# Seven row blocks of each feed-forward output projection computed as 2x2 block products with seven multiplications (Strassen's scheme, Winograd's form), block sums on GpSimd

## The reference, cut to what matters

```python
D_MODEL, D_FF, SEQ = 1024, 2816, 256

def swiglu(x, w_in, w_out):
    gate, up = jnp.split(x @ w_in, 2, axis=-1)
    return (jax.nn.silu(gate) * up) @ w_out

for i in range(2):
    h = h + 0.5 * swiglu(rmsnorm(h, norm_g[i, 0]), ffn_w_in[i, 0], ffn_w_out[i, 0])
    h = h + mixer(rmsnorm(h, norm_g[i, 1]))        # mixer_a for i = 0, mixer_b for i = 1
    h = h + 0.5 * swiglu(rmsnorm(h, norm_g[i, 2]), ffn_w_in[i, 1], ffn_w_out[i, 1])
return rmsnorm(h, final_g)
```

## Time and profile before

| | before |
|---|---|
| median of 3 runs | 1740.37 us (1740.19 to 1740.73) |
| span of the profiled execution | 1738.4 us |
| outside the span, against the median | 2.0 us |
| PE busy | 1722.3 us, 99% |
| DVE busy | 870.7 us, 50% |
| ACT busy | 659.1 us, 38% |
| POOL busy | 37.3 us, 2% |
| granted PE clock, mean | 0.998 |

### The profile page before, as it was taken

How to read it: one execution, slowest core, us unless ns; L and a number is a source line. 1 busy time by engine, 2 the same in 40 slices (tenths; PEclk the granted TensorE clock), 3 DMA queues, 4 the chain that set the end, 5 groups by cost and what they waited for, 6 DMA issues and landing times.

```text
span 1738.4 us, 21080 instructions
## 1 busy us (share of the span) xinstructions
PE 1722.3 (99%) x9024; PEld 1294.2 (74%) x9024; DVE 870.7 (50%) x1138; ACT 659.1 (38%) x831; POOL 37.3 (2%) x64
## 2 busy tenths in 40 slices
PE   9999999999999999999999999999999999999998
PEld 7988744444444458888998888888888899888887
DVE  6876411111111146554686555465546688565554
ACT  5555311111111144443335444344434444444442
POOL 2010000000000000000000000000001000000000
PEclk9999999999999999999999999999999999999999
DMA  9738999999999995554743555545556654545551
GB/s 357 215 129 315 356 409 427 428 429 429 425 431 425 426 391 198 194 185 140 265 146 113 196 187 194 193 183 193 181 186 220 220 188 146 191 172 206 183 183 46
DMA packets 50756, 439.02 MB, mean 253 GB/s; under 512 B 6368, under 2 KB 6764, under 8 KB 11616
## 3 DMA queue, kind: packets, MB, share of 16 engines
q1 hardware_dynamic: 46640, 425.17, 64.0%
q0 software_dynamic: 3792, 12.15, 2.5%
q10 hardware_dynamic: 224, 0.29, 0.0%
HBM read 434.37 MB, written 3.15 MB: 252 GB/s over the span
## 4 chain that ended last, share of the span: by engine, by line
PE 96%; DMA 1%; DVE 1%; issue 1%; ACT 1%; POOLq 0%; POOL 0%; DVEq 0%; ACTq 0%
PE PS L629 22%; PE PS L631 22%; PE PS L630 22%; PE PS L1874 18%; PE PS L1841 3%; PE PS L1932 2%; DMA ujug<-in_wt 1%; PE PS L2581 1%; PE PS L668 1%; PE PS L3115 1%; PE PS L1912 1%; PE PS L2723 0%; DMA ki<-ki 0%; PE PS L1006 0%; PE PS L2759 0%
## 5 line engine op out<-in xcount | busy, mean ns | idle before, releaser
L587 DVE TENSOR_TENSOR wl<-ring,wh 128x2048 fp32r<-128x2048 f32 (+1 forms) x207 | 470.1, 2273 | 284.7 <-ACT wh L578 284.5
L578 ACT ACTIVATE wh<-ring 128x2048 fp32r<-128x2048 f32 (+1 forms) x207 | 393.5, 1902 | 274.5 <-PE PS L631 274.5
L629 PE MATMUL PS<-wh,XTh 128*128 128x512 f32 x952 | 378.3, 397 | 1.9 <-DVE wl L623 0.6
L631 PE MATMUL PS<-wh,XTl 128*128 128x512 f32 x952 | 371.5, 390 | 0.0
L630 PE MATMUL PS<-wl,XTh 128*128 128x512 f32 x952 | 371.0, 390 | 0.0
L629 PEld LDWEIGHTS PS<-wh,XTh 128*128 128x128 f32 x952 | 178.8, 188 | 39.3 <-issue 1.2
L631 PEld LDWEIGHTS PS<-wh,XTl 128*128 128x128 f32 x952 | 178.7, 188 | 38.2
L630 PEld LDWEIGHTS PS<-wl,XTh 128*128 128x128 f32 x952 | 179.0, 188 | 35.1 <-issue 0.2
L629 PE MATMUL PS<-XTh,wh 128*128 128x256 f32 (+2 forms) x480 | 137.8, 287 | 0.1
L629 PE MATMUL PS<-wh,hTh 128*128 128x512 f32 x352 | 137.6, 391 | 0.0
L631 PE MATMUL PS<-wh,hTl 128*128 128x512 f32 x352 | 137.1, 389 | 0.0
(11 more groups left out here) (460 smaller groups left out, 1913.4 us busy)
## 6 DMA issues: line engine op xcount, KB each, us to landing
ring<-in_wt SPq DMA_DIRECT2D x205, 1024.0 KB, 4.9
ubuc<-in_wt SPq DMA_DIRECT2D x6, 4096.0 KB, 22.8
uf<-in_wt SPq DMA_DIRECT2D x20, 1024.0 KB, 20.4
uhui<-in_wt SPq DMA_DIRECT2D x5, 4096.0 KB, 24.3
ujug<-in_wt SPq DMA_DIRECT2D x5, 4096.0 KB, 21.4
uaue<-in_wt SPq DMA_DIRECT2D x5, 4096.0 KB, 23.6
uaue<-in_wt SPq DMA_DIRECT2D x9, 2048.0 KB, 21.3
ud<-in_wt SPq DMA_DIRECT2D x9, 2048.0 KB, 23.8
```

The lines of the kernel that those rows point to most:

```text
L578: s.activation(k.pieces(i)[0], k.raw(i), ACT.Copy).then_inc(*k.w_hi.up(i))
L587: v.tensor_tensor(l, k.raw(i), h.bitcast(F32), ALU.subtract).then_inc(*k.w_lo.up(i))
L629: pe.matmul(o, lhsT=left[0], rhs=right[0], start=first, stop=False)
L631: return pe.matmul(o, lhsT=left[1], rhs=right[0], start=False, stop=final)
```

## The change

Of the eleven parts of each output projection, parts 1 to 7 (`QUADS`) are computed as one 2 x 2 block product: left the two halves of the tokens by the two blocks of 128 rows, right the part cut into four blocks of 128 x 512. Seven products take the place of eight. For this

- the host packs the four blocks of such a part in another order (`quad`); the part is as large as before,
- GpSimd makes four sums of the right blocks (`sum_blocks`: one instruction over 128 x 1024, two over 128 x 512, each waiting for the one before) into one of two places `sums0`, `sums1`; the third and later of a stage wait until the sums two before have been split,
- ACT and DVE split three of the four blocks (1536 columns instead of 2048) and all the sums (another 2048): two items, which take two of the three split places in turn (`items`),
- GpSimd makes four sums of the left blocks (`sum_forms`, 128, 256 and 128 columns), and ACT and DVE split seven forms of 128 columns instead of four blocks (896 columns instead of two times 256),
- the seven products go to the four old banks and to four more, which had held gate and up (`quad_banks`), and are collected there over the seven parts,
- before the tail ACT copies one of the four new banks and DVE adds all of them into X with six instructions (`quad_scalar`, `quad_vector`),
- the place of a quad part in the ring is free only when its sums are done too (`load_part`),
- the DMA scratch of the software queue is set to 4096 bytes, which makes room in SBUF.

```diff
+QUADS = (1, 2, 3, 4, 5, 6, 7)
+    def quad(name, at, r0):
+        parts.append((1, 2048, [(name, at, r0 + r, c, c + 512) for r, c in ((0, 512), (0, 0), (128, 0), (128, 512))]))
...
+    def items(self, i):
+        return [i, ("sums", i)] if i in self.quads else [i]
...
     if j is not None:
         sp.wait_ge(*(k.w_used if j in k.expert else k.w_lo).at(j))
+        if j in k.quads:
+            sp.wait_ge(*k.w_sum.at(("t4", j)))
...
-    s.wait_ge(*k.landing(i).at(i))
-    s.activation(k.pieces(i)[0], k.raw(i), ACT.Copy).then_inc(*k.w_hi.up(i))
+    s.wait_ge(*(k.w_sum.at(("t4", i[1])) if isinstance(i, tuple) else k.landing(i).at(i)))
+    s.activation(k.pieces(i)[0], k.to_split(i), ACT.Copy).then_inc(*k.w_hi.up(i))
...
-    v.tensor_tensor(l, k.raw(i), h.bitcast(F32), ALU.subtract).then_inc(*k.w_lo.up(i))
+    v.tensor_tensor(l, k.to_split(i), h.bitcast(F32), ALU.subtract).then_inc(*k.w_lo.up(i))
...
+def sum_blocks(g, k, i, used):
+    b, t = k.raw(i).rearrange("p (n c) -> p n c", c=512), k.sums_of(i).rearrange("p (n c) -> p n c", c=512)
+    if used is not None:
+        g.wait_ge(*k.w_lo.at(used))
+    g.wait_ge(*k.landing(i).at(i))
+    g.tensor_tensor(t[:, 0:2, :], b[:, 0:1, :].broadcast_to([128, 2, 512]), b[:, 1:4:2, :], ALU.subtract).then_inc(
+        *k.w_sum.up(("t1", i)))
+    g.wait_ge(*k.w_sum.at(("t1", i)))
+    g.tensor_tensor(t[:, 2, :], b[:, 3, :], t[:, 0, :], ALU.subtract).then_inc(*k.w_sum.up(("t2", i)))
+    g.wait_ge(*k.w_sum.at(("t2", i)))
+    g.tensor_tensor(t[:, 3, :], b[:, 2, :], t[:, 2, :], ALU.subtract).then_inc(*k.w_sum.up(("t4", i)))
...
+def ffn_gpsimd(g, k, m, i):
+    for c in QUADS:
+        sum_forms(g, k, m, c)
+    for n, p in enumerate(QUADS):
+        sum_blocks(g, k, i + 22 + p, ("sums", i + 22 + QUADS[n - 2]) if n >= 2 else None)
...
     for p in range(1, 8):
-        deep_step(pe, k, i + p, k.hT, p, 22, h)
+        if p in QUADS:
+            quad_step(pe, k, m, i + p, p, h)
+        else:
+            deep_step(pe, k, i + p, left, p, 22, h)
...
+def quad_step(pe, k, m, i, p, h):
+    pe.wait_ge(*k.w_lo.at(i))
+    b = k.blocks(i)
+    product(q[0], 4, b, 0, first, final)
+    product(h, 5, b, 1, False, False)
+    product(h + 1, 3, b, 2, False, False).then_inc(*k.w_used.up(i))
+    pe.wait_ge(*k.w_lo.at(s))
+    b = k.blocks(s)
+    product(h + 2, 6, b, 3, False, False)
+    product(q[1], 0, b, 0, first, final)
...
+    product(q[2], 2, b, 2, first, final)
+    product(q[3], 1, b, 1, first, final).then_inc(*k.w_used.up(s))
...
     for p in range(8):
-        split_lo(v, k, k.after[i + p])
+        for x in k.items(i + p):
+            split_lo(v, k, k.after[x])
+    quad_vector(v, k, m, i + QUADS[-1], h)
     tail_vector(v, k, m, i + 10, h, nxt, 0.5)
...
-        nc = _bacc.Bacc("TRN2", target_bir_lowering=False, num_devices=1)
+        nc = _bacc.Bacc("TRN2", target_bir_lowering=False, num_devices=1,
+                         dynamic_dma_scratch_size=4096)
```

More of the change, by code:

```diff
@@ L118, in ffn @@
             pair("ffn_w_in_2", (i, j), 256 * c, 2816 + 256 * c, 256)
-        for c in range(6):
-            deep("ffn_w_out_2", (i, j), 512 * c, min(4, 22 - 4 * c))
+        for p in range(11):
+            if p in QUADS:
+                quad("ffn_w_out_2", (i, j), 256 * p)
+            else:
+                deep("ffn_w_out_2", (i, j), 256 * p, 2)
     def joined(name, at, spans):
@@ L276, in __init__ @@
         self.part_at = [0] + list(itertools.accumulate(128 * nk * w for nk, w, _ in self.parts))
-        split = [i for i in range(len(self.parts)) if i not in self.expert]
+        down = [self.at[n] + 22 for n in ("f0", "f1", "f2", "f3")]
+        self.quads = [i + p for i in down for p in QUADS]
+        split = [x for i in range(len(self.parts)) if i not in self.expert for x in self.items(i)]
         self.buffer, self.left, self.after, self.extra = split_plan(split, self.at["a_out"])
@@ L390, in __init__ @@
         self.hr = here("hr", 1024, 4, 256)
-        self.hT = (here("hTh", 2048, 22, 256, dtype=F32R), here("hTl", 7680, 22, 256, dtype=F32R))
+        n_h = 512 * (11 - len(QUADS)) + 896 * len(QUADS)
+        self.h_at = list(itertools.accumulate([896 if c in QUADS else 512 for c in range(10)], initial=0))
+        self.hT = (here("hTh", 2048, n_h, dtype=F32R), here("hTl", 2048 + n_h, n_h, dtype=F32R))
+        self.forms = here("forms", 20912, 8, 128)
+        self.sums = (here("sums0", 18864, PART), here("sums1", 21936, PART))
+        self.mixed = self.forms.rearrange("p a b -> p (a b)")
         self.xg_ = here("xg_", 18864, 2, 1024)
@@ L443, in col, with sums_of, quad_at, pair_of @@
         return self.gcol[:, o:o + n]
+    def items(self, i):
+        return [i, ("sums", i)] if i in self.quads else [i]
+    def sums_of(self, i):
+        return self.sums[QUADS.index(self.quad_at(i)) % 2]
+    def quad_at(self, i):
+        return next(i - self.at[n] - 22 for n in ("f3", "f2", "f1", "f0") if i >= self.at[n])
+    def pair_of(self, c, t):
+        o = self.h_at[c]
+        return [x[:, o:o + 512].rearrange("p (k i) -> p k i", i=256)[:, :, 128 * t:128 * t + 128] for x in self.hT]
+    def forms_of(self, c):
+        return [x[:, self.h_at[c]:self.h_at[c] + 896].rearrange("p (f i) -> p f i", i=128) for x in self.hT]
+    def to_split(self, i):
+        if isinstance(i, tuple):
+            return self.sums_of(i[1])
+        return self.raw(i)[:, 512:2048] if i in self.quads else self.raw(i)
     def raw(self, i):
@@ L2599, in ffn_tensor, with left @@
     i += 22
[L2600 removed]
+    def left(kk, t):
+        return [x[:, kk % 2, :] for x in k.pair_of(kk // 2, t)]
+    deep_step(pe, k, i, left, 0, 22, h)
     turn(10, turn_banks(k, m, h, 10))
     for p in range(1, 8):
[L2603 to L2605 removed]
+        if p in QUADS:
+            quad_step(pe, k, m, i + p, p, h)
+        else:
+            deep_step(pe, k, i + p, left, p, 22, h)
+    deep_tail(pe, k, m, i, left, 22, h, nxt)
 def ffn_vector(v, k, m, i, h, nxt):
     def turn(c, b):
+        if c in QUADS:
+            hi, lo = k.forms_of(c)
+            v.wait_ge(*m.s.at(f"fh{c}"))
+            v.tensor_tensor(lo, k.forms[:, 1:8, :], hi.bitcast(F32), ALU.subtract).then_inc(*m.v.up(f"tl{c}.1"))
+            return
         for t in T:
[L2612 removed]
+            hi, lo = k.pair_of(c, t)
             v.wait_ge(*m.s.at(f"th{c}.{t}"))
@@ L2621, in ffn_vector @@
             split_lo(v, k, k.after[i + 2 * c])
+        if c - 1 in QUADS:
+            turn(c - 1, turn_banks(k, m, h, c - 1))
         for t in T:
@@ L2648, in ffn_scalar @@
             split_hi(s, k, k.after[i + 2 * c])
+        if c - 1 in QUADS:
+            forms(c - 1)
         if c == 0:
@@ L2661, in ffn_scalar @@
     for p in range(8):
-        split_hi(s, k, k.after[i + p])
+        for x in k.items(i + p):
+            split_hi(s, k, k.after[x])
+    quad_scalar(s, k, m, i + QUADS[-1], h)
     tail_scalar(s, k, m, i + 10, h, nxt)
@@ L2673, in deep_step, with quad_banks, product @@
                 kk = 2 * p + j
-                mm = rows_of(pe, k.bank(h + 2 * t + nn), xt, kk, t, w, j, 512 * nn, 512 * nn + 512, kk == 0,
-                             kk == nk - 1)
+                mm = three(pe, k.bank(h + 2 * t + nn), xt(kk, t), [x[:, j, 512 * nn:512 * nn + 512] for x in w], kk == 0,
+                           kk == nk - 1)
     mm.then_inc(*k.w_used.up(i))
+def quad_banks(k, m, h):
+    return [k.gate_bank(m, h, c, t) for c in (10, 9) for t in T]
+def quad_step(pe, k, m, i, p, h):
+    q, first, final = quad_banks(k, m, h), p == QUADS[0], p == QUADS[-1]
+    a, s = k.forms_of(p), ("sums", i)
+    def product(bank, form, blocks, n, start, stop):
+        return three(pe, k.bank(bank), [x[:, form, :] for x in a], [x[:, n, :] for x in blocks], start, stop)
+    pe.wait_ge(*k.w_lo.at(i))
[7 more added lines that the diff above has]
+    product(q[1], 0, b, 0, first, final)
+    if first:
+        pe.wait_ge(*m.v.at("tl10.1"))
+    product(q[2], 2, b, 2, first, final)
+    product(q[3], 1, b, 1, first, final).then_inc(*k.w_used.up(s))
@@ new lines, in quad_scalar, with quad_vector @@
+def quad_scalar(s, k, m, i, h):
+    s.wait_ge(*k.w_used.at(("sums", i)))
+    s.activation(k.mixed[:, 0:512], k.bank(quad_banks(k, m, h)[0]), ACT.Copy, scale=0.5).then_inc(*m.s.up("p1"))
+def quad_vector(v, k, m, i, h):
+    q, X = quad_banks(k, m, h), k.X
+    u2, u3 = k.mixed[:, 512:1024], k.sums_of(i)[:, 0:512]
+    v.wait_ge(*m.s.at("p1"))
+    v.scalar_tensor_tensor(u2, k.bank(q[2]), 0.5, k.mixed[:, 0:512], ALU.mult, ALU.add).then_inc(*m.v.up("u2"))
+    v.scalar_tensor_tensor(X[:, 0, 512:1024], k.bank(q[1]), 0.5, X[:, 0, 512:1024], ALU.mult, ALU.add).then_inc(
+        *m.v.up("c12"))
+    v.scalar_tensor_tensor(X[:, 1, 512:1024], k.bank(q[1]), 0.5, X[:, 1, 512:1024], ALU.mult, ALU.add).then_inc(
+        *m.v.up("c22"))
+    v.wait_ge(*m.v.at("u2"))
+    v.scalar_tensor_tensor(u3, k.bank(q[3]), 0.5, u2, ALU.mult, ALU.add).then_inc(*m.v.up("u3"))
+    v.wait_ge(*m.v.at("c12"))
```

(7 more changed lines are left out.)

36 lines of the change are left out of this document (29 added, 7 removed).

## The result

The changed kernel takes 1792.1 us (median of 4 runs, 1790.9 to 1793.1) against 1740.3 in the same comparison: the ratio is 1.030, 95% interval 1.0288 to 1.0314. It is slower by 3%, 7 us under the forecast of 1799 and by the forecast's mechanism.

A forecast was written before the change was run, and what follows sets the result against it. PE was taken to bound the kernel everywhere. With splits and block sums excluding each other, 1738.4 + 57.2 (projections) + 1.8 (tail) = 1797.4, plus 2.0 us outside the span: 1799 us, range 1719 to 1824.

The forecast's parts named there:

- What bounds, what is removed: PE bounds the kernel everywhere; a quad part takes 21 matmuls, 4.76 us instead of 5.44, saving 19.0 us over 28 parts.
- GpSimd's price: GpSimd's block sums cost 5.0 us per quad part, the geometric middle between 2.60 and 9.6.
- The hold: A DVE split with two SBUF inputs and GpSimd block sum exclude each other for their whole length; chance 0.60.
- The projection's sum: Part 7 of each projection ends at 58.3 us instead of 44.0, losing 14.3 us a stage, 57.2 in four.
- PE's idle time: In the projections PE waits for delayed splits; its idle time goes from none to about 21 us a stage.
- The tail: Six new DVE instructions after part 10's split make PE 0.6 us late in three stages, 1.8 us.
- At nothing: No cost from the sums' claim on ring places, the small DMA scratch, or the left forms in the first phase.
- The other side: Rival 2: DVE's splits and GpSimd's block sums run at once, all is hidden, 1723 us; chance 0.28.

The follow-up runs named there:

- four in a row: Changed kernel with only `QUADS` changed, to parts 1 to 4 instead of seven, sums still on GpSimd: 1761.2 us, 1.0125.
- four parts with gaps and a place more: Changed kernel with quad parts only 1, 2, 5 and 7, sums on GpSimd, and a third place for sums: 1731.3 us, 0.9951; repeated 1730.8 us, 0.9954.
- the five-part run: Changed kernel with quad parts only 1, 2, 4, 5 and 7 and block sums on DVE instead of GpSimd: 1738.3 us, 0.9999.

## Why the prediction was right

**What bounds, what is removed.** Right. Without the sums 28 quad parts and the tail give 1738.4 - 1721.4 = 17.0 us of span; the working has 19.0 less 1.8.

**GpSimd's price.** 5.0 us a group was a geometric middle between 2.6 and 9.6 and is 5.03 measured. That the figure was so close is luck of the method; that it lay between the two ends was not. The Trainium skill ("GPSIMD Engine Reference", section 3.1) gives 4497 ns for 2048 columns. No run here has that size on GpSimd; the 2048 columns of a group take 5.03 us in three instructions, and 1024 in one take 2.42, a little more than half of the skill's figure.

**The hold.** Right, by the runs with one SBUF input and with fills, which part it in all three ways: two inputs beside a reading GpSimd 1792, one input 1727, a GpSimd that only writes 1723. The rule of the Trainium skill ("SBUF — State Buffer", section "Who interferes with whom") agrees in each. Why L1451 was not held is not shown: that a GpSimd instruction which reads only four numbers gives nothing to be held by is the prediction's argument, and no run tried it.

**The projection's sum.** It was 14.3 us a stage; in f0 it is 12.6 us. ACT, released by the last use of part 7, starts the split that stood at 807.49 here:

```profile
820.14 1.92 ACT L624 ACTIVATE wh<-ring 128x2048 fp32r<-128x2048 f32 x1 [1.88 <-PE PS L711]
```

The term that is off is the round, 9.05 us in the working (5.0 + 4.05) and 8.48 measured. The measured lengths give 5.03 + 4.05 = 9.08; a round changes four times from one engine to the other, and each change gives 0.14 to 0.15 us back, 0.6 in all. From the start of sums 3 (768.43) to the end of sums 7 (809.97 + 2.69 = 812.66) lie 44.2 us where the working had 47.1, 2.9 less. Sums 3 started 5.2 us after part 0's start at 763.2 instead of 4.3, which takes 0.9 back, and the last splits and matmuls, to 820.14, took 7.5 instead of 6.9, which takes 0.6.

**PE's idle time.** The 21 us a stage do not follow from the working: a stage that ends at 58.3, with 39.2 of PE's own, leaves 19.1. Measured are 12.5 us of waits. The other part is PE itself, slower after a wait. The kernel without sums runs the same 8940 matmul records in 1703.7 us of busy time, the changed one in 1724.0, 20.3 us more, 5.1 a stage. The span's growth closes by these rows: -19.0 + 50.0 + 1.6 + 20.3 = 52.9, measured 1791.2 - 1738.4 = 52.8. In the seven-part kernel PE's slowness itself costs next to nothing in f0: PE starts behind its waits at 791.84, 800.32 and 808.79, 8.48 and 8.47 apart, though the matmuls of the first of these rounds take 1.5 us longer than those of the second: the wait behind them is shorter by as much (1.81 against 3.35). With four in a row the last and longest wait of a stage has none behind it, and what PE loses there counts.

**The tail.** Right: 1.8 us forecast, 1.6 in three waits of 0.5 (PE on `xg_`).

**At nothing.** Right for the forms, ring places and DMA scratch: the kernel without sums has all three and its waits are those of before plus the tail's. PE's wait on `ki` went from 1.6 to 1.2.

**The other side.** The 1723 forecast for two engines that run at once is met where nothing reads beside the splits (1722.9, 1723.3). With real sums beside splits of one input it is 1727.2: a group takes 5.2 us there, over PE's 4.76, and that it would be hidden up to 5.6 was a little too much.

## What to carry to other kernels

An engine that is idle is no room for work until one knows what it shares: here GpSimd was at 2% and DVE at 50%, but a float32 subtraction with both inputs in SBUF and a GpSimd instruction that reads SBUF take turns, so their times add, less 0.15 us at each turn, and 4.05 + 5.03 us do not fit under 4.76. Add up the time of both engines as if they were one and set it against the bound engine's for each stretch, not for the kernel. Where the sum is over it, spread the work (four parts with gaps and a place more gave 0.9951) or do it on the faster of the two (four parts, 0.9961; seven, 1.0069 instead of 1.0301). Read the price of an operation from its minimum and the collision from the distance of the median to it.

## What the hardware showed that I had not expected

After some of its waits PE ran at half its pace for a few us. PE's timeline of the changed kernel in f0:

```profile
791.84 0.51 PE L709 MATMUL PS<-wh,hTh 128*128 128x512 f32 x1 [3.35 <-DVE wl L633]
792.18 0.40 PE L710 MATMUL PS<-wl,hTh 128*128 128x512 f32 x1
...
793.16 0.63 PE L710 MATMUL PS<-wl,hTh 128*128 128x512 f32 x1
793.59 0.63 PE L711 MATMUL PS<-wh,hTl 128*128 128x512 f32 x1
...
795.72 0.49 PE L710 MATMUL PS<-wl,hTh 128*128 128x512 f32 x1
796.06 0.39 PE L711 MATMUL PS<-wh,hTl 128*128 128x512 f32 x1
```

and the stretches around it (busy us and count of PE, weight loads, DVE, ACT, POOL; then the granted clock):

```profile
780.00:786.00 6.00, 4.94 (x23) 3.74 (x21) 6.00 (x2) 1.49 (x1) 5.84 (x3) 1.00 0.40 164
792.00:798.00 6.00, 6.00 (x20) 4.76 (x21) 2.79 (x2) 2.20 (x2) 5.92 (x3) 0.72 0.16 35
798.00:804.00 6.00, 4.19 (x19) 3.03 (x18) 5.04 (x2) 1.10 (x1) 5.84 (x3) 1.00 0.33 139
```

The clock was granted at 0.72 in the mean of the middle stretch, a mixture of its two levels, 1.2 and 2.4 GHz: starts 0.43 us apart are the lower, 0.227 the upper. Of the nine waits of over 3 us in the changed kernel's projections eight were followed by such a stretch, of 7 or 8 matmuls at the lower level; the 15 waits of 0.95 to 1.8 us were not.

The length of a wait does not decide it alone. With four in a row the clock fell behind two of four waits of 3.15 to 3.17 us and stayed at 1.00 behind the other two. With five parts and sums on DVE all four waits are 1.77 to 1.78 us, and it fell behind one; with six, behind two of four of 1.9. The stretches of six us that hold the four waits of the five-part run:

```profile
780.00:786.00 6.00, 5.39 (x24) 4.46 (x25) 5.93 (x5) 0.78 (x1) 0.00 (x0) 1.00 0.71 262
1097.00:1103.00 6.00, 5.16 (x23) 4.27 (x24) 5.93 (x5) 1.01 (x1) 0.00 (x0) 1.00 0.69 227
1283.00:1289.00 6.00, 5.03 (x15) 4.02 (x16) 5.96 (x4) 1.15 (x1) 0.00 (x0) 0.72 0.61 191
1687.00:1693.00 6.00, 5.76 (x25) 4.79 (x26) 5.93 (x5) 0.41 (x1) 0.00 (x0) 1.00 0.77 244
```

With seven parts and sums on DVE, 16 waits of 1.24 to 1.37 us, it never fell. What else decides it stays open.
